# The context group's experts in fours instead of pairs, in a two-layer diffusion backbone on one core

## What is computed

```python
def block(args):
    x_i, i_i, g_i = args                      # 128 tokens, their 128 expert indices and weights
    u = jnp.take(u_tab, i_i, axis=0)
    a = jax.nn.gelu(jnp.einsum('td,thkd->thk', x_i, u))
    return jnp.einsum('thk,thkd->td', a * g_i, jnp.take(v_tab, i_i, axis=0))
```

## Time and profile before

| | |
|---|---|
| median of 3 runs | 4802.89 us (4797.89 to 4812.7) |
| the profiled execution's own time | 4810.34 us |
| its span | 4808.5 us |
| busy: PE, DVE, POOL, ACT | 79%, 69%, 38%, 32% of the span |
| mean DMA rate | 334 GB/s |
| granted clock of TensorE, mean | 0.912 |
| dots of the prompt's experts, first to last start | 542.8 to 1179.1 us, and 2734.4 to 3411.5 us |

### The profile page before, as it was taken

How to read it: one execution, slowest core, us unless ns; L and a number is a source line. 1 busy time by engine, 2 the same in 40 slices (tenths; PEclk the granted TensorE clock), 3 DMA queues, 4 the chain that set the end, 5 groups by cost and what they waited for, 6 DMA issues and landing times.

```text
span 4808.5 us, 42013 instructions
## 1 busy us (share of the span) xinstructions
PE 3781.9 (79%) x12514; PEld 2031.1 (42%) x12514; DVE 3304.2 (69%) x7685; ACT 1544.1 (32%) x4530; POOL 1828.8 (38%) x1515
## 2 busy tenths in 40 slices
PE   7987789896797666767867679889699777777776
PEld 4547464445453233323533346445554332322222
DVE  2323788768898976666567778867889876755555
ACT  2311241101244334444333323110134444444443
POOL 2330132243344434444344323224244444444443
PEclk8989899998899888988898889999799999999999
DMA  7665377676899989999999757757599999999998
GB/s 271 211 215 210 133 277 279 257 290 244 323 415 407 378 335 401 416 411 388 381 420 419 284 223 268 310 206 288 227 380 412 401 416 419 410 417 421 422 421 346
DMA packets 231551, 1604.70 MB, mean 334 GB/s; under 512 B 27590, under 2 KB 29938, under 8 KB 42908
## 3 DMA queue, kind: packets, MB, share of 16 engines
q0 software_dynamic: 198016, 1395.87, 72.8%
q1 hardware_dynamic: 33308, 206.16, 11.0%
HBM read 1590.62 MB, written 11.30 MB: 333 GB/s over the span
## 4 chain that ended last, share of the span: by engine, by line
PE 33%; DMA 30%; DVE 24%; issue 6%; ACT 5%; POOL 3%; SPq 0%; ACTq 0%; DVEq 0%; POOLq 0%
DMA sb_arena<-in_peer_uv,sb_idx 14%; DMA sb_gbufs<-in_peer_uv,sb_idx 13%; PE ps L1149 12%; PE ps L1045 7%; DVE sb_gbufs L1965 5%; DVE sb_arena L1965 3%; DVE sb_eacc L1988 3%; PE ps L1086 3%; PE ps L726 2%; PE ps L753 2%; DMA sb_ring<-in_w_oab 1%; POOL sb_gbufs L2208 1%; ACT sb_small L1419 1%; DVE sb_arena L1951 1%; DVE sb_arena L1953 1%
## 5 line engine op out<-in xcount | busy, mean ns | idle before, releaser
L2208 POOL DMA_INDIRECT sb_gbufs<-in_peer_uv,sb_idx x768 | 1002.0, 1305 | 1748.0 <-DVE sb_eacc L1988 765.7
L1149 PE MATMUL ps<-sb_gbufs,sb_dge 128*128 128x512 f32 x1792 | 893.1, 648 | 279.6 <-ACT sb_dge L1440 274.3
L1149 PE MATMUL ps<-sb_arena,sb_dge 128*128 128x512 f32 x1792 | 891.4, 648 | 263.1 <-ACT sb_dge L1440 263.0
L2208 POOL DMA_INDIRECT sb_arena<-in_peer_uv,sb_idx x512 | 625.6, 1222 | 757.9 <-PE ps L1149 641.1
L1965 DVE CUSTOM_DVE_ANT_0 sb_gbufs<-sb_gbufs,sb_keep 128x1024 f32<-128x1024 f32 x512 | 625.7, 1234 | 367.5 <-DMA sb_gbufs<-in_peer_uv,sb_idx 365.7
L1965 DVE CUSTOM_DVE_ANT_0 sb_arena<-sb_arena,sb_keep 128x1024 f32<-128x1024 f32 x512 | 622.1, 1229 | 326.2 <-DMA sb_arena<-in_peer_uv,sb_idx 324.3
L1149 PEld LDWEIGHTS ps<-sb_gbufs,sb_dge 128*128 128x128 f32 x1792 | 353.9, 206 | 781.1 <-ACT sb_dge L1440 387.2
L1149 PEld LDWEIGHTS ps<-sb_arena,sb_dge 128*128 128x128 f32 x1792 | 354.8, 206 | 767.1 <-issue 386.1
L1416 ACT ACTIVATE sb_small<-sb_small 128x2 f32<-128x2 f32 x512 | 104.1, 203 | 1511.0 <-DVE sb_small L1965 1506.0
L1988 DVE SCALAR_TENSOR_TENSOR sb_eacc<-sb_gbufs,sb_small,sb_eacc 128x1024 f32<-128x1024 f32 x315 | 412.4, 1309 | 8.0 <-issue 0.3
L1965 DVE CUSTOM_DVE_ANT_0 sb_gbufs<-sb_gbufs,sb_h2p 128x1024 f32<-128x1024 f32 x256 | 316.6, 1255 | 61.9 <-DMA sb_gbufs<-in_peer_uv,sb_idx 61.7
(11 more groups left out here) (274 smaller groups left out, 4342.3 us busy)
## 6 DMA issues: line engine op xcount, KB each, us to landing
sb_ring<-in_w_wq SPq DMA_DIRECT2D x48, 1024.0 KB, 8.9
sb_keep<-in_w_ada POOLq DMA_DIRECT2D x52, 512.0 KB, 6.2
sb_ring<-in_w_hy SPq DMA_DIRECT2D x24, 1024.0 KB, 7.2
sb_ring<-in_w_oab SPq DMA_DIRECT2D x18, 1024.0 KB, 7.4
sb_ring<-in_w_ga SPq DMA_DIRECT2D x16, 1024.0 KB, 9.8
sb_ring<-in_w_gb SPq DMA_DIRECT2D x16, 1024.0 KB, 7.1
sb_ring<-in_w_out SPq DMA_DIRECT2D x14, 1024.0 KB, 8.8
sb_gbufs<-in_peer_uv,sb_idx POOLq DMA_INDIRECT x768
```

Source lines behind the costliest of these rows:

```text
L1149: q = pe.matmul(ps[:, c, :], dge[:, b, :], gbuf[b][:, D + c * 512:D + c * 512 + 512], start=(h == 0 and i == 0), stop=(h == HALVES - 1 and ...
L2208: nc.gpsimd.indirect_dma_start(out=gbuf[b], out_offset=None, in_=I["peer_uv"], in_offset=bass.IndirectOffsetOnAxis(ap=idx[:, col:col + 1], ...
```

## The change

The rounds of the prompt go by fours. The constants become `QUAD` = 4, `QUADS` = 32 and `UNITS` = 8. On DVE eight units hold the four sums of the four before, then the four dots, with one set of small operations (128x4) behind the fourth dot. ACT's tanh is over four columns and stands in the eighth unit, and the column index is `q = 4 * (m % 2)`. POOL issues four gathers in the first four units of the eight and none in the other four. The buffers are the same four, and a gather still waits for the sum that frees its buffer. The units of a layer are 8 * 33 = 264. Nothing else differs.

```diff
--- before.py
+++ after.py
@@ -24,8 +24,9 @@
 GROUPS = NB // HALF
 TOKEN = 4 // HALF
 HALVES = SLOTS // HALF
-PAIRS = SLOTS // 2
-UNITS = 4
+QUAD = 4
+QUADS = SLOTS // QUAD
+UNITS = 2 * QUAD
 STEPS_S = (TILES - 1) * HALVES
 TOKENS_S, TOKENS = STEPS_S // TOKEN, HALVES // TOKEN
 WIDTHS = [TOPK // (i + 1) for i in range(TOPK)]
@@ -301,7 +302,7 @@
         pace = GR[1].pace()
         wq = len(pace) - 2 * (NHP + 1)
         end = sum(pace[:wq]) / sum(pace)
-        order = spread(pace, 0 if layer else 5, UNITS * (PAIRS + 1), end - 0.005)
+        order = spread(pace, 0 if layer else 5, UNITS * (QUADS + 1), end - 0.005)
         if layer == 0:
             for k, n in ((4, 1), (3, 2), (2, 2), (1, 3)):
                 order[k:k] = ["R0"] * n
@@ -1131,7 +1132,7 @@
 
             def expert_step(group, layer):
                 if group == "p":
-                    for _ in range(UNITS * (PAIRS + 1)):
+                    for _ in range(UNITS * (QUADS + 1)):
                         yield
                     return
                 for b in (0, 1):
@@ -1398,12 +1399,12 @@
 
             def expert_step(group, layer):
                 if group == "p":
-                    for m in range(PAIRS):
-                        q = 2 * (m % 4)
+                    for m in range(QUADS):
+                        q = QUAD * (m % 2)
                         for _ in range(UNITS - 1):
                             yield
-                        act.wait_ge(Z["inner"], layer * PAIRS + m + 1)
-                        act.activation(dth[:, q:q + 2], din[:, q:q + 2], ACT.Tanh, scale=GELU_C).then_inc(Z["th_p"], 1)
+                        act.wait_ge(Z["inner"], layer * QUADS + m + 1)
+                        act.activation(dth[:, q:q + QUAD], din[:, q:q + QUAD], ACT.Tanh, scale=GELU_C).then_inc(Z["th_p"], 1)
                         yield
                     for _ in range(UNITS):
                         yield
@@ -1991,29 +1992,31 @@
 
             def expert_step(group, layer):
                 if group == "p":
-                    def finish_pair(m):
-                        q = 2 * (m % 4)
-                        dve.wait_ge(Z["th_p"], layer * PAIRS + m + 1)
+                    def finish_quad(m):
+                        q = QUAD * (m % 2)
+                        dve.wait_ge(Z["th_p"], layer * QUADS + m + 1)
                         dve.wait_ge(Z["p_small"], smalls[0])
-                        link(dve.scalar_tensor_tensor(out=dw[:, q:q + 2], in0=dth[:, q:q + 2], scalar=1.0, in1=dgate[:, q:q + 2], op0=ALU.add, op1=ALU.mult))
-                        for i in (0, 1):
-                            add_value("p", layer, 2 * m + i, q + i, m == 0 and i == 0)
+                        link(dve.scalar_tensor_tensor(out=dw[:, q:q + QUAD], in0=dth[:, q:q + QUAD], scalar=1.0, in1=dgate[:, q:q + QUAD],
+                                                      op0=ALU.add, op1=ALU.mult))
+                        for i in range(QUAD):
+                            add_value("p", layer, QUAD * m + i, q + i, m == 0 and i == 0)
                             yield
 
-                    for m in range(PAIRS):
-                        q = 2 * (m % 4)
+                    for m in range(QUADS):
+                        q = QUAD * (m % 2)
                         if m:
-                            yield from finish_pair(m - 1)
+                            yield from finish_quad(m - 1)
                         else:
+                            for _ in range(QUAD):
+                                yield
+                        for i in range(QUAD):
+                            dot("p", layer, QUAD * m + i, q + i, h2p[:, :])
+                            if i == QUAD - 1:
+                                gelu_argument(q, QUAD, gwt[:, QUAD * m:QUAD * m + QUAD])
                             yield
-                            yield
-                        dot("p", layer, 2 * m, q, h2p[:, :])
-                        yield
-                        dot("p", layer, 2 * m + 1, q + 1, h2p[:, :])
-                        gelu_argument(q, 2, gwt[:, 2 * m:2 * m + 2])
-                        yield
-                    yield from finish_pair(PAIRS - 1)
-                    yield
+                    yield from finish_quad(QUADS - 1)
+                    for _ in range(QUAD - 1):
+                        yield
                     dve.wait_ge(Z["acc"], added[0])
                     link(dve.tensor_tensor(eacc, eacc, g2[:, 0, :], ALU.mult))
                     m = dve.tensor_tensor(x[:, 0, :], x[:, 0, :], eacc, ALU.add)
@@ -2212,11 +2215,12 @@
                 if group == "p":
                     for n in range(4):
                         gather("p", layer, n)
-                    for m in range(PAIRS + 1):
-                        if 1 <= m < PAIRS - 1:
-                            for n in (2 * m - 2, 2 * m - 1):
-                                gather("p", layer, n + 4)
+                    for m in range(QUADS + 1):
+                        if 1 <= m < QUADS:
+                            for n in range(QUAD * (m - 1), QUAD * m):
+                                gather("p", layer, n + QUAD)
                                 yield
+                            for _ in range(QUAD):
                                 yield
                         else:
                             for _ in range(UNITS):
```

## The result

The changed kernel takes 5001.61 us (median of 4 runs, 4986.64 to 5011.75), the kernel before 4807.8 us beside it. The ratio is 1.0395, with a 95% interval of 1.0373 to 1.0417: slower by 179 to 201 us. The profiled execution has a span of 4996.3 us against 4808.5, so 188 us more.

A forecast was written before the change was run, and what follows sets the result against it. PE and DVE were taken to hold each other, with the gather loop only just hidden. Loss of 147 us on short fours less 15 gives +132 us on the 4802.9 us median: 4935 us, range 4835 to 5040.

The forecast's parts named there:

- the loop theory: Prompt's experts: the way from a freed buffer through gather and landing to its dot sets the time; forecast +132 us.
- The period of 20.5 us for four: Experts' loop: smallest time for four experts, summed from issue, landings, dot, small operations, sum and dense step: 20.5 us.
- The first landing: First gather of a four, from POOL's issue to landing: taken as 6.4 us, the shortest in the rows.
- the distance of two landings: Gathers of one four: successive landings taken 3.3 us apart, three such distances making 9.9 us.
- The loss on the short fours, 147 us: Both layers: 38 of 62 periods were under 20.5 us, and what they are short of it sums to 147 us.
- The long fours, taken as a gain of 15 us: 24 fours long enough for the loop gain about 1.2 us each, half of it on the path: 15 us.
- Behind the experts, taken as nothing: Stage of the latent group's experts, after the prompt's: moved later by the delay but as long as before.
- Where the first layer ends: Last dot of the first layer some 65 us later than 1179; the second layer adds as much.
- Removed work, 45 us of operations and 32 of round trips as a bound of 77: DVE: 64 sets of small operations and half the tanh waits go; at most 77 us gained if all on the path.
- Rival A (early landings): First landing some 4.4 us, others 2.4 apart, period 15.8 us, so no waits left: 4743 us; chance 0.08.
- Rival B (DVE's idle time takes the waits): New waits only replace DVE's idle time, 97 us against losses of 78 in three stretches: about 4805 us; chance 0.07.

The follow-up runs named there:

- the fours without gathers: Changed kernel with the gathers of the prompt's experts left out from the fifth round on, so part of the computation is missing: 4732.1 us, ratio 0.9835.
- the split halves: Changed kernel with each prompt gather as two, a u half freed by the dot and a v half freed by the sum: 4777.36 us, ratio 0.9922.
- The two runs that moved the dense steps there: Changed kernel with a four's dots, small operations, tanh and sums in one unit: 5057.68 us; with only the dots together in the eighth unit: 5025.65 us.
- the runs without gathers: Kernel before (pairs) and changed kernel (fours), each without the prompt's gathers from the fifth round on: 4754.86 us and 4732.1 us.
- the split ones: Changed kernel and kernel before (pairs), each prompt gather split into separately freed u and v halves: 4777.36 us and 4794.77 us.
- the clumped fours: Changed kernel with four dots, small operations, tanh and four sums in one unit, seven empty units behind: 5057.68 us, ratio 1.0510.
- the clumped ones without gathers: Changed kernel with each four's dots, small operations, tanh and sums in one unit, prompt gathers left out from the fifth round on: 4936.26 us, ratio 1.0247.

## Why the prediction was right, and by how much it fell short

- **Direction and mechanism: right.** The loop from freed buffer to landing became the bound. With the transfers gone the change gains 23 us; with the u half freed early it gains as well. Both are the loop theory's, and no rival of the prediction explains both.
- **The period of 20.5 us for four: right.** The changed kernel has 40 dots in 200 us (20.0 us; forecast 39), and the second layer's 20 and 19 dots in 100 us are 20.0 and 21.1. The first landing (6.3 us median by the landing records, 6.4 taken) and the distance of two landings (3.2 median, 3.3 taken) are as put; the mean distance is 3.8, and the median period of the 62 fours 20.9 us. The row of the Hyena stretch shows the parts otherwise distributed: 8.2 us for the first (776.99 to 785.16) and 2.5 for the next two.
- **The loss on the short fours, 147 us: nearly right.** The 38 fours that took less than 20.5 us before take 156 us more.
- **The long fours, taken as a gain of 15 us: wrong.** This is the step that failed. I held that a four longer than the loop hides it. The 24 fours of 20.5 us and more did not get shorter; together they take 17 us more, and their dots wait some 105 of the 315 us for gathers. It costs 32 us against the forecast. That the gathers do it is shown: the same 24 fours, counted in the same way, are 55 us shorter than before in the fours without gathers and 36 us shorter with the split halves. Why a long four does not hide the loop is my reading: it is long because a block of dense work stands somewhere in it, and the landing is hidden only if that block stands between the sums and the dots. The two runs that moved the dense steps there speak for it. In them these 24 fours are 30 and 29 us shorter than before, while the 38 short ones take 261 and 235 us more and swamp the sum. The moved steps changed other waits too, so this part stays argued.
- **Behind the experts, taken as nothing:** 18 us, from the last dot of the second layer to the end. 14 of them are the block of dense work that now stands behind the last dot, because that dot stands eight units before the end and not four; the runs without gathers and the split ones have the same two distances, 1.0 us before the last dot with pairs and 12.9 behind it with fours, so it is the order of the units. It is a piece of the old stretch that my count from dot to dot did not reach, rather than new work. The other 5 I can't place.
- **Where the first layer ends:** I had its last dot some 65 us later and as much in the second layer; it is 93 us later (1271.7 against 1179.1), and the second layer is 75 us longer. The loss of the first layer was the larger one, not an equal part.
- Forecast +132, measured +190 or so: 9 on the short fours, 32 on the long ones and 18 behind make the difference.
- **Removed work, 45 us of operations and 32 of round trips as a bound of 77:** the wait for the tanh fell by 35 us, as put. About 23 us of it all reach the end in the runs without gathers, and 17 in the pair of split kernels.
- **Rival A (early landings):** its price of 4.4 us for a landing, and with it the figure of the Trainium skill (DMA: Bandwidth & Descriptors, Anatomy of one DMA), is not what the runs show: 6.3 us at 1.05 MB and 5.1 at 0.52 MB. The slope, 1.2 us for 0.52 MB, agrees with the page's 436 GB/s, the fixed part does not (4 us here by my estimate and about 2 there).
- **Rival B (DVE's idle time takes the waits):** DVE's idle time in 600 to 800 us rose from 28.7 to 63.4 us instead of being used up. 25.5 of these 34.7 us are the dots' waits for gathers, 35.5 us in the rows above against 10.0 before:

```profile
DVE sb_gbufs L1965 <- DMA sb_gbufs<-in_peer_uv,sb_idx: 10.0, 5, 4.2
```

So the new waits came on top of the old idle time; DVE did not catch up.

- **What I had not priced: TensorE's clock.** PE is busy 169.1 us at 0.81 in 600 to 800 us where it was 175.7 at 0.93. What a slower PE can have cost directly is bounded by its busy time as the page has it, 40 us more in the whole program for the same matmuls, about a fifth of the 188; the other 148 us are PE standing idle. How much of that idle time goes back to the slower clock, these runs do not separate.

## What to carry to other kernels

When several small steps are grouped, ask what the group holds while it is collected: here the four buffers, so that the loads lost a third of their time and all went out at once. Write the loop down, from the release of a buffer to the next use of its data, and compare its sum with the period by stretches; the mean over the program (61.7 us of waits in 4808) did not show how near the edge the old loop was. And look for a part of the buffer that is free earlier: releasing the u half at the dot turned 190 us of loss into a gain of 37.

## What the runs showed that I had not expected

- The place of an engine's work matters as much as its amount. The same operations, in one run of 12 us instead of spread over eight units, cost 204 us with no transfer in the way.
- TensorE's granted clock followed: 0.97, 0.81, 0.71 and 0.68 in 600 to 800 us for the fours without gathers, the change, the clumped fours and the clumped ones without gathers.
- Doubling the number of gathers and halving each could be afforded: POOL's busy time in 600 to 800 us went from 68 to 132 us of 200, DMA moved 296 GB/s against 294, and the fours came out 37 us ahead. Some 40 us of cost stayed against the runs without gathers, and the doubling may be part of it.
- An operation of 128x4 takes what one of 128x2 does, 0.16 to 0.18 us, and so does the tanh on ACT (205 and 203 ns at the median).
